# One opening stage, norms by a power and a diagonal matrix, and a convolution inside the projection's eviction, in a three-layer kernel on one core

## The reference

```python
def rmsnorm(x, g):
    y = x * rsqrt(mean(x * x, axis=-1) + EPS)
    return y * g
mem_h = rmsnorm(mem, mem_norm)                     # mem: 256 x 1024
for layer in range(2):
    h = rmsnorm(x, mix_norm[layer])
    mkv = mem_h @ mem_w_kv[layer]                  # 1024 -> 256 key and 256 value columns
    mem_k = rmsnorm(mkv[:, :256] by heads of 64, mem_k_gain[layer]); mem_v = mkv[:, 256:]
    # layer 0:
    z = h @ a_w_in                                 # 3*768 convolution columns, 256 query columns
    gate_b, gate_c, u = split(z[:, :2304], 3)
    y_tok = gate_b * causal_conv3(gate_c * u, conv_w)
    q = rmsnorm(z[:, 2304:] by heads of 64, mem_q_gain) / 8
    x = x + concat([y_tok, attention(q, mem_k, mem_v)]) @ w_out[layer]; x = x + mlp(rmsnorm(x, mlp_norm))
```

## Time and profile before

| | |
|---|---|
| time of the runs, median (lowest to highest) | 2101.14 us (2100.75 to 2101.48) |
| profiled execution, its own time | 2103.42 us |
| its span | 2101.6 us |
| mean granted PE clock | 0.904 |
| PE busy | 1727.1 us (82%) |
| DVE busy | 899.9 us (43%) |
| ACT busy | 553.9 us (26%) |
| POOL busy | 29.3 us (1%), 19 instructions |
| moved by DMA | 380.42 MB, mean 181 GB/s |

### The profile page before, as it was taken

One profiled execution on the slowest core, in us unless ns is written; L12 is line 12 of the kernel. 1 busy time (PEld: TensorE's weight loads), 2 busy tenths in 40 slices (PEclk: granted clock), 3 DMA queues, 4 the chain that ended last, 5 costly groups with the idle time before them and its releaser, 6 DMA issues. The chain is left out here.

```text
span 2101.6 us, 31455 instructions
## 1 busy us (share of the span) xinstructions
PE 1727.1 (82%) x13427; PEld 1267.5 (60%) x13427; DVE 899.9 (43%) x1413; ACT 553.9 (26%) x779; POOL 29.3 (1%) x19
## 2 busy tenths in 40 slices
PE   3786899876668999895787996959859999889885
PEld 1485799754446999795686884547644434333432
DVE  1445555322545554586665455645552111111111
ACT  1323444211343444324102103444321111110111
POOL 0000000000000000001300000000000000000000
PEclk9897999987668999896899998989969999999998
DMA  6320745332004655250000333325169999999994
GB/s 236 121 81 23 289 168 192 108 123 85 1 1 178 223 200 199 101 180 11 2 4 3 120 123 141 140 101 191 36 226 334 394 393 394 394 394 393 394 392 154
DMA packets 170971, 380.42 MB, mean 181 GB/s; under 512 B 9814, under 2 KB 20306, under 8 KB 170078
## 3 DMA queue, kind: packets, MB, share of 16 engines
q1 hardware_dynamic: 169166, 378.15, 49.2%
q10 hardware_dynamic: 1680, 0.43, 0.1%
HBM read 377.43 MB, written 1.14 MB: 180 GB/s over the span
## 5 line engine op out<-in xcount | busy, mean ns | idle before, releaser
L1194 DVE TENSOR_TENSOR mlp_w_lo<-weight_slots,mlp_w_hi 128x2048 fp32r<-128x2048 f32 x64 | 143.8, 2288 | 59.2 <-ACT mlp_w_hi L1164 59.2
L2602 PE MATMUL ps<-weight_slots,moe_h 128*64 128x512 f32 x512 | 148.5, 624 | 21.8 <-DMA weight_slots<-in_w_exp_up 11.6
L2602 PE MATMUL ps<-moe_slots,moe_h 128*64 128x512 f32 x512 | 148.1, 623 | 17.4 <-DMA moe_slots<-in_w_exp_up 14.8
L135 PE MATMUL ps<-mlp_h_hi,mlp_w_hi 128*128 128x256 f32 x512 | 145.1, 283 | 2.5 <-DVE mlp_w_lo L1194 2.5
L137 PE MATMUL ps<-mlp_h_hi,mlp_w_lo 128*128 128x256 f32 x512 | 145.0, 283 | 0.0
L136 PE MATMUL ps<-mlp_h_lo,mlp_w_hi 128*128 128x256 f32 x512 | 145.0, 283 | 0.0
L1164 ACT ACTIVATE mlp_w_hi<-weight_slots 128x2048 fp32r<-128x2048 f32 x64 | 119.7, 1910 | 58.4 <-PE ps L137 47.9
L2680 DVE TENSOR_TENSOR moe_hidT<-moe_silu,ps 128x256 f32<-128x256 f32 x32 | 13.5, 421 | 281.5 <-ACT moe_silu L2639 281.5
L2602 PEld LDWEIGHTS ps<-weight_slots,moe_h 128*64 128x64 f32 x512 | 48.7, 143 | 99.8 <-issue 98.1
L2602 PEld LDWEIGHTS ps<-moe_slots,moe_h 128*64 128x64 f32 x512 | 49.5, 143 | 94.7 <-issue 92.4
L135 PEld LDWEIGHTS ps<-mlp_h_hi,mlp_w_hi 128*128 128x128 f32 x512 | 98.3, 192 | 4.7 <-DVE mlp_w_lo L1194 4.2
(11 more groups left out here) (590 smaller groups left out, 3775.8 us busy)
## 6 DMA issues: line engine op xcount, KB each, us to landing
weight_slots<-in_w_in SPq DMA_DIRECT2D x20, 2048.0 KB, 7.7
weight_slots<-in_w_up SPq DMA_DIRECT2D x16, 2048.0 KB, 9.0
weight_slots<-in_w_down SPq DMA_DIRECT2D x16, 2048.0 KB, 7.8
weight_slots<-in_w_exp_gate SPq DMA_DIRECT2D x16, 2048.0 KB, 19.7
weight_slots<-in_w_exp_up SPq DMA_DIRECT2D x16, 2048.0 KB, 22.4
moe_slots<-in_w_exp_up SPq DMA_DIRECT2D x16, 2048.0 KB, 22.1
moe_slots<-in_w_exp_down SPq DMA_DIRECT2D x16, 2048.0 KB, 19.4
moe_slots<-in_w_exp_gate SPq DMA_DIRECT2D x16, 2048.0 KB, 19.4
```

What stands on the lines that cost most here:

```text
L135: pe.matmul(dst, left[0], right[0], start=start, stop=False, skip_group_check=inside)
L1194: dve.tensor_tensor(piece_slot(w_split[1], jj), raw_piece(jj), piece_slot(w_split[0], jj).bitcast(F32), ALU.subtract).then_inc(w_lo, 1)
L2602: mm = pe.matmul(ps[side(kind), 0, :], h_sel[:, k, :], w[kind][:, k, :], start=(k == 0), stop=(k == KD - 1))
```

## The change

There are five parts.

1. `setup`, `norm("mem")`, `memory`, `late_loads` and `norm("n0")` become one stage, `opening`. It has its own semaphore for each kind of load. Ten of the seventeen small vectors are issued by POOL, `x` is loaded ahead of the first weight unit, and the next units are requested as soon as a unit is used.
2. Every norm takes the power -0.5 on POOL (`ALU.pow` against a constant tile) instead of a root on ACT and a reciprocal on DVE. The factor 1/D moves into the squares.
3. `norm` no longer scales the tokens. DVE makes a diagonal matrix of the factors for each token tile, and PE multiplies the unscaled block by it, so that the turn and the scaling are one plain matmul. The loop runs chunk by chunk with both tiles inside.
4. In `a_in` the query jobs come before the last two chunks, DVE evicts all jobs from the sixth on, and the convolution of a chunk is done when its last factor is evicted. The query norm is there too, its power on POOL.
5. The queries and the keys of layer 1 are turned in one stage (`mem_turns`); the keys of layer 0 inside `opening`. The SSD norm works by token tile, and in `final_norm` ACT and DVE square one tile each.

```diff
+    parts["minus_half"] = np.full((P, 32), -0.5)
...
-        def setup(mem, rows, table, hb):
+        def opening(mem, rows, table, hb, kn, kv, sq, st):
                 @block.gpsimd
+                    for tile, r, n, src in on_pool:
+                        pool.dma_start(rows[r:r + n, tile, :], src).then_inc(rows_landed, 16)
+                    pool.wait_ge(const_in, 16)
+                    for i in range(2):
+                        pool.wait_ge(squares, NT * (i + 1))
+                        pool.tensor_scalar(stat[:, i, 0, :], stat[:, i, 0, :], EPS, None, ALU.add).then_inc(added, 1)
+                        pool.wait_ge(added, i + 1)
+                        pool.tensor_tensor(stat[:, i, 1, :], stat[:, i, 0, :], c_("minus_half")[:, 0:NT], ALU.pow)\
+                            .then_inc(rooted, 1)
...
                 @block.sync
+                    for tile, r, n, src in on_sp:
+                        sp.dma_start(rows[r:r + n, tile, :], src).then_inc(first_rows, 16)
+                    sp.dma_start(x[:, :, :], a["x"][0].rearrange("(t p) d -> p t d", p=P)).then_inc(x_in, 16)
...
+                    stream.prefetch(sp, u0 + 2)
...
         def norm(name, src, outs, scaled=None, sync=None):
-                        act.wait_ge(scale, 1)
-                        act.activation(stat[:, 2, :], stat[:, 1, :], ACT.Sqrt).then_inc(roots, 1)
...
-                        dve.wait_ge(roots, 1)
-                        dve.reciprocal(stat[:, 3, :], stat[:, 2, :]).then_inc(scale, 1)
-                        dve.wait_ge(scale, 2)
+                        dve.wait_ge(rooted, 1)
                         for t in range(NT):
-                            dve.tensor_scalar(scaled[:, t, :], src[:, t, :], stat[:, 3, t:t + 1], None, ALU.mult)\
+                            dve.tensor_scalar(diag[:, t, :], ident, stat[:, 1, t:t + 1], None, ALU.mult)\
                                 .then_inc(scale, 1)
...
-                                mm = pe.transpose(ps[:, c, t * P:(t + 1) * P], scaled[:, t, c * P:(c + 1) * P], ident)
...
+                                mm = pe.matmul(ps[:, c, t * P:(t + 1) * P], src[:, t, c * P:(c + 1) * P], diag[:, t, :],
+                                               start=True, stop=True)
+                            mm.then_inc(turned, 1)
...
+                def convolve(dve, c, bank, chain):
+                    chain(dve.tensor_tensor(gc[:, c, :], gc[:, c, :], bank[:, 0:S], ALU.mult))
+                    chain(dve.tensor_scalar(gu[:, c, :], gc[:, c, :], col("conv_w", 2 * nconv + c), None, ALU.mult))
+                    for tap in (1, 0):
+                        back = 2 - tap
+                        chain(dve.scalar_tensor_tensor(gu[:, c, back:], gc[:, c, 0:S - back],
...
+                    return dve.tensor_tensor(cat[:, c, :], gb[:, c, :], gu[:, c, :], ALU.mult)
...
                 def consume(eng, j, bank, chain, vector):
...
+                    if c >= q_job:
+                        chain(query_norm(eng, c - q_job, chain))
+                    return convolve(eng, c - 2 * nconv, bank, chain)
...
+                split_stage("a_in", units, consume, hT, on_vector=lambda j: j >= nconv, on_pool=query_roots)
```

More of the change, by code:

```diff
@@ L630, in _ @@
[L630 to L635, removed]
+                    sp.dma_start(mem[:, :, :], a["mem"][0].rearrange("(t p) d -> p t d", p=P)).then_inc(mem_in, 16)
+                    sp.dma_start(const[:, :], a["const"]).then_inc(const_in, 16)
@@ L651, in _ @@
-                    act.dma_start(table[0:NBK, :], a["rel_bias"]).then_inc(landed, 16)
-                    n += 2
+                        .then_inc(small_in, 16)
+                    act.wait_ge(mem_in, 16)
+                    act.activation(squared[:, 0, :], mem[:, 0, :], ACT.Square, scale=D ** -0.5,
+                                   accum_out=stat[:, 0, 0, 0:1]).then_inc(squares, 1)
+                    act.wait_ge(cols_out, 1)
+                    for c in range(1, KD, 2):
+                        act.wait_ge(mem_turned, c + 1)
+                        act.activation(hT[:, c, :], ps[:, c, 0:S], ACT.Copy, scale=col("mem_norm", c)).then_inc(memT_a, 1)
@@ L654, in _, with turn_rows @@
                 @block.tensor
                 def _(pe):
[L656 to L672, removed]
+                    def turn_rows(i, bank, c0):
+                        pe.transpose(ps[:, bank, c0:c0 + P], rows[:, i, :], ident).then_inc(rows_turned, 1)
@@ new lines, in _ @@
+                    pe.wait_ge(memT_v, KD // 2)
+                    pe.wait_ge(memT_a, KD // 2)
+                    project_memory(0)
+                    pe.wait_ge(rows_landed, 16 * len(on_pool))
+                    turn_rows(1, 4, 0)
+                    turn_rows(2, 5, 0)
+                    pe.wait_ge(table_in, 16)
+                    pe.matmul(ps[0:NH, 6, :], table[0:NBK + 1, :], c_("hot")[0:NBK + 1, :],
+                              start=True, stop=True).then_inc(rows_turned, 1)
+                    for j in range(1, 2 * NT):
+                        project_memory(j)
@@ new lines, in conv_layer, with turn @@
+                split_stage("a_in", units, consume, hT, on_vector=lambda j: j >= nconv, on_pool=query_roots)
+                qT = sb("mq_T", [P, MW // P, S], on=on)
+                def turn(pe, j, bank):
+                    of, pair = divmod(j, MW // P)
+                    for t in range(NT):
+                        src = (qn[:, t], kn[:, 1, t])[of]
+                        mm = pe.transpose(bank[:, t * P:(t + 1) * P], src[:, pair * P:(pair + 1) * P], ident)
+                    return mm
@@ L1281, in conv_layer @@
+                stage("mem_turns", 2 * MW // P, turn, lambda eng, j, bank, chain, vector:
+                      copy(eng, vector, (qT[:, j] if j < 2 else mem_kT[:, 1, j - 2]), bank[:, 0:S]))
+                attention("mem_attn0", [memory_item(0, t, qT, nconv, [(1, 2, 4)]) for t in range(NT)], cat)
                 add_projection("out0", unit["out0"], cat)
@@ L1303, in memory_item @@
                 empty=empty)
-        def memory_attention(layer, q, cat, chunk0):
-            with ExitStack() as on:
-                qT = sb("mq_T", [P, MW // P, S], on=on)
-                memory_queries(layer, q, qT)
-                attention(f"mem_attn{layer}", [memory_item(layer, t, qT, chunk0, [(1, 2, 4)]) for t in range(NT)], cat)
         def shared_buffers(on):
@@ L2251, in ssd @@
                 sums, scaled, rooted = sem("sn_sums"), sem("sn_scaled"), sem("sn_rooted")
[L2252 removed]
+                st = sb("ssd_st", [P, 2, NT, SG], on=on)
                 junk = xs
```

400 lines of the change are left out of this document (254 added, 146 removed).

## The result

The changed kernel takes 2076.9 us (median of four runs, 2074.57 to 2079.72); the kernel before, measured beside it, 2101.31 us. The ratio is 0.9882, with a 95% interval from 0.987 to 0.9893. The gain is 24.4 us where 40.4 were forecast, and the time lies above the range of 2051 to 2071. The profiled execution took 2079.72 us, the slowest of the four, with a span of 2077.9 us; against the profiled execution of before it gains 23.7. All that follows compares these two.

What follows compares the result with a forecast made beforehand. PE is busy 82% of the span, but a chain through one engine after another binds the opening. Terms -28.1 - 0.3 - 0.6 - 8.4 - 2.5 - 0.5 = -40.4 gave 2061 us, range 2051 to 2071.

Steps and rivals of the forecast that it cites:

- Opening: From the kernel's start to `a_in`: projection waits only for the first weight unit, `a_in` starts at 60.5, not 88.62; -28.1 us.
- the rival of a late POOL: At the start: POOL's ten loads, of a price not seen, delay the projection by up to 3.5 us; 2064, chance 10%.
- End of a_in: Convolution and query norm inside `a_in`'s eviction: the attention starts at 159.9, not 168.29; -8.4 us.
- Power: POOL's replacement of root and reciprocal: 0.36 us add, 0.45 power, 0.25 handovers, together 1.06.
- The rival of dear powers: A power costs 1 to 1.5 us, some ten stand one behind another; 2066 to 2071, chance 12%.
- Norms: Four exposed norms (two MLPs, n2, n4), diagonal products in 5.5 us with the clock rising 4 us in; sum -0.3 us.
- the rival whose clock stays at half: Clock stays at half through the four norms: 1.4 us longer each, n2's successor starts slow, 7.3 in all; 2068, chance 17%.
- the gain I booked behind n2: The stage following n2: its first 3.4 us at half clock become 1.7 at full clock; -1.7 us.
- theory B: From the experiments, not the prediction: lost gain is chance, the clock falling and rising by where in time a stage lies.
- the clock gives nothing there: Behind the MLP norms: DVE's low part holds the MLP until 229.53, so a faster clock changes nothing; 0 us.
- The reason that the prediction gives for the early rise: In the norms: transpose-mode turns do not count as work for the fast clock, plain products do and raise it.
- The end: Last norm: factors ready at 2093.9, not 2095.57, but the gain vector lands 3.6 us after issue, at 2095.1; -0.5 us.

Runs made afterwards that it cites:

- the norms as before: Changed kernel with the norms of the two MLPs, n2, n4 and n5 back to root, reciprocal, scaling and turns; 2071.01 us, ratio 0.9863.
- the better parts together: Changed kernel with head norms by root and reciprocal, and other norms scaling on DVE and turning, their factor from POOL's power; 2064.96 us, ratio 0.9826.
- the extra matmuls: Changed kernel with three extra matmuls of x with the identity at the head of each MLP, results overwritten; 2069.68 us, ratio 0.9846.
- The turns with the power's factor: Changed kernel with norms scaling on DVE and turning with the identity, the factor still from POOL's add and power; 2069.87 us, ratio 0.9855.

## Why the prediction was wrong

**Opening, right.** -27.4 was measured for -28.1: the weights came 1.2 us later than taken, and 0.5 of it was won back. POOL was done early, so the rival of a late POOL fell.

**End of a_in, right.** -8.7 was measured for -8.4. Putting it back cost 10.7, of which 1.4 is the query norm's power of 8 elements (its stage took 5.1 us, 3.8 before).

**Power, the step that failed.** "I take 0.36 for the add, 0.45 for the power": add and power of 2 elements took 0.22 and 0.72, a pair with its handovers 1.15 instead of 1.06. That was near enough for the norms, and wrong for the head norms, where I used the same number for 24 elements and wrote "+0.5" for two query norms that cost +5.2, and "-1.1" for keys that cost +0.3 in their stage. No row of before had a power in it: the 0.36 was an add of 8 elements and the 4.87 a product of 2048, and between those two the step from 2 to 24 elements costs next to nothing, so one price went to every size. The rival of dear powers named the right operation and had a wrong shape: it too gave one price to every power. By 0.4 + 0.158 n the two query norms would have come to +5.4 (+5.2 was measured, and the root and reciprocal put back took 5.2 off again), and the SSD norm, with two powers of 4 (1.01 each), to -1.4 instead of -2.5; -1.6 was measured. The keys are less clear: with their root put back the stage took 6.86 us in one kernel and 6.40 in another, so no run shows what the powers alone cost there.

**Norms, half right.** For the MLPs' norms -1.0 was measured for -1.2. In n2 and n4 PE began where I had it, within 0.2 us, but its clock rose 5.5 us into the products (4.05 in the two MLPs), not 4, so the products took 6.4 and not 5.5, nearer to the 6.9 of the rival whose clock stays at half. And the gain I booked behind n2, -1.7, did come: the compression's first matmuls ran at full clock. It was lost again at 417.2, 0.9 us behind a wait of PE of 3.3 us:

```profile
416.30:417.10 0.80, 0.79 (x4) 0.44 (x5) 0.00 (x0) 0.80 (x1) 0.00 (x0) 1.00 1.07 385
417.30:420.60 3.30, 3.30 (x10) 1.29 (x9) 0.00 (x0) 0.26 (x1) 0.00 (x0) 0.50 0.19 69
```

Before, the same wait of 3.3 us was followed by no fall, and none follows in the norms as before. Still, the products are not needed for it: the clock falls there in all seven profiles with the products, and also in the better parts together, which has turns, between 413.7 and 417.1 us, and there the compression took 46.1 us instead of 44.7. So this fall is not pinned to the products, and theory B may be right for it. For the MLPs I wrote "the clock gives nothing there". It took 1.5 us each: at full clock PE was done with x after 3.67 us instead of 5.17, so that it idled 2.80 us instead of 1.30 ahead of the first matmul of the weights, and the fall then met matmuls that bind. This is the second step that failed, +3.0, shown by the extra matmuls and by the turns.

The reason that the prediction gives for the early rise doesn't hold as it stands. It leans on the Trainium skill (TensorE: Matmul & The Clock Gate, "Part 4: PE-mode transpose"), by which a turn doesn't count as work for the fast clock, and n2's rows of before agreed. The turns with the power's factor disagree. In n2 there PE was idle for 6.0 us, did nothing but turns from 381.72, and the clock was up 2.9 us later:

```profile
381.70:384.60 2.90, 2.88 (x14) 2.88 (x15) 1.29 (x3) 0.45 (x2) 0.00 (x0) 0.50 0.00 0
384.65:388.00 3.35, 0.96 (x7) 0.70 (x6) 2.52 (x7) 2.53 (x7) 0.00 (x0) 1.00 0.00 0
```

The same is seen at other norms of the kernels with turns, though at none of the kernel before. What differs for certain is that 16 products last twice as long as 16 turns at the same clock; whether their kind matters too, no run separates.

**What I left at zero.** The first attention with its projection +1.5, the projection of the NSA queries +0.5, the NSA attention +1.7, the stretch behind the SSD norm +0.7, the experts -2.4: none of these has an edit. For the two attentions a lower clock is measured beside the longer time. For the others the cause is open: the experts took 536.4 to 540.7 us over the changed kernels, and the stretch behind the SSD norm 145.1 to 145.4 in every one of them, which does not look like chance. A forecast of this kernel that holds such stages at zero is wrong by some 3 us, by these rows.

**The end.** The final norm's gain vector took 4.1 us to land where I took 3.6, and was issued at 2067.7, at the start of the stage. It is what the last pass waits for, and nothing was won.

By the sum, the terms of the powers account for 7.0 of the 16.7 us between forecast and result (keys 1.4, queries 4.7, SSD norm 0.9), those of the norms' products and the clock behind them for 6.7 (MLPs 3.0, n2 and compression 2.6, n4 1.1), and the opening, the end and the stages at zero for the remaining 3.0. Experiments show 4.7 of the first and, for the second, the MLPs' 3.0 and the longer n2 and n4; the keys, the SSD norm and the compression's fall are argued from the profiles.

## What to carry to other kernels

Price an operation by the elements of the one that you replace, not by the smallest of its kind: a power of 2 elements is cheaper than a root behind a table load, one of 24 costs 3.7 us more than root and reciprocal. Before you put plain matmuls in place of turns, look at what PE does behind them: here the clock rose early, PE then idled 2.8 us, and the clock fell on work that binds; three extra matmuls in the wait cured it. And undo a change part by part: here some of its parts gave 36 us and the others took 11 back.

## What the runs showed of the hardware

- A power on POOL takes about 0.4 us and 0.158 us more for each element of a partition's row (0.70 for 2, 1.64 for 8, 4.16 for 24, 5.43 for 32), on 32 partitions the same as on 128.
- Beside a pass of DVE over 1024 elements with two operands (1.28 us) POOL's product of 2 elements took 1.27 us instead of 0.20, and the power of 4 took 1.93 instead of the 1.01 of the SSD norm, in the second and third row of the windows above. The Trainium skill (SBUF — State Buffer, "Terms") says that the two engines share a pair of ports that one of them holds for a whole instruction; these rows agree. In the changed kernel the keys' norm pays a little for it: one power of 4 elements took 1.17 us there, and the two adds of 4 elements 0.38 and 0.47 instead of the 0.20 of `a_in`.
- Turns alone can raise the clock: behind 6.0 us of idle PE it went from 0.50 to 1.00 2.9 us after the first of 16 turns, in n2 of the kernel with the power and without the products. They don't always: in the kernel before it stayed at 0.50 through the turns of all seven norms.
- A plain fp32 product of 128 by 128 leaves two records and takes twice the time of a turn of the same size at the same clock (6.4 us for 16, with the last 0.9 us at full clock, against 3.7 at half clock).
- POOL issues a small load in 0.50 to 0.54 us (its first took 0.77), SP in 0.33 to 0.5.
